# States renewed within the scan, turned states through the weight ring, twelve expert tiles loaded ahead, the light expert two blocks late, and packed weights

## The reference

```python
def mamba2(h, conv_buf, ssm_h, w_in, ...):
    proj = h @ w_in
    z = proj[..., :D_INNER]
    xbc, conv_new = causal_conv(proj[..., D_INNER:D_INNER + CONV_DIM], conv_buf, conv_w, conv_b)
    ...
    y, h_new = ssd(xs, dt, a_neg, bm, cm, ssm_h)      # chunked scan, per sequence state 32 x 64 x 128
    y = rmsnorm((y + d_skip[:, None] * xs).reshape(b, l, D_INNER) * jax.nn.silu(z), norm_g)
    return y @ w_out, conv_new, h_new
def moe(h, w_router, w_gate, w_up, w_down):           # 8 experts, D_MODEL 1024, D_FF_EXPERT 2816
    ...
    for e in range(N_EXPERTS):
        y = y + combine[..., e:e + 1] * swiglu(h, w_gate[e], w_up[e], w_down[e])
```

## Time and profile before

| | |
|---|---|
| median of 3 runs | 1618.4 us (1617.58 to 1619.77) |
| the profiled execution: time, span | 1623.92 us, 1622.1 us |
| TensorE busy | 1530.0 us (94%) |
| VectorE, ScalarE, GpSimd busy | 381.1, 277.4, 108.4 us |
| DMA traffic | 454.83 MB, mean 280 GB/s |
| expert stage, from the first expert product to the last | 909.84 to 1602.8 us |

### The profile page before, as it was taken

How to read it: one execution, slowest core, us unless ns; L and a number is a source line. 1 busy time by engine, 2 the same in 40 slices (tenths; PEclk the granted TensorE clock), 3 DMA queues, 4 the chain that set the end, 5 groups by cost and what they waited for, 6 DMA issues and landing times.

```text
span 1622.1 us, 24833 instructions
## 1 busy us (share of the span) xinstructions
PE 1530.0 (94%) x10024; PEld 906.4 (56%) x10024; DVE 381.1 (23%) x928; ACT 277.4 (17%) x618; POOL 108.4 (7%) x187
## 2 busy tenths in 40 slices
PE   7999988999999999999999999999999989998998
PEld 3545544678888878858787554553244234432342
DVE  2233422120000045644557300001000100011014
ACT  2122332110000022337612200000001000000001
POOL 0002424000000010011010200001000100010000
PEclk9999999899999999989999999999999999999999
DMA  9676972444433564564359999999999999999996
GB/s 373 268 239 238 395 234 71 156 125 137 155 110 123 182 194 134 156 204 142 92 200 369 320 337 374 390 398 392 414 403 417 395 411 406 418 394 406 411 411 223
DMA packets 195915, 454.83 MB, mean 280 GB/s; under 512 B 21870, under 2 KB 109963, under 8 KB 177845
## 3 DMA queue, kind: packets, MB, share of 16 engines
q1 hardware_dynamic: 181760, 406.07, 67.7%
q0 software_dynamic: 11536, 46.00, 8.2%
q10 hardware_dynamic: 2512, 1.23, 0.3%
HBM read 437.91 MB, written 15.55 MB: 280 GB/s over the span
## 4 chain that ended last, share of the span: by engine, by line
PE 80%; DMA 11%; DVE 5%; issue 2%; ACT 1%; SPq 0%; POOLq 0%; POOL 0%; DVEq 0%; ACTq 0%
PE bank L1056 11%; PE bank L1086 10%; PE bank L1546 9%; PE bank L1596 6%; DMA ring<-in_moe_w_up 6%; PE bank L1100 5%; PE bank L1439 5%; DMA ringx<-in_moe_w_up 3%; PE bank L1134 3%; PE bank L789 3%; PE bank L1454 2%; PE bank L1480 2%; PE bank L1558 2%; PE bank L823 2%; PE bank L876 1%
## 5 line engine op out<-in xcount | busy, mean ns | idle before, releaser
L1546 PE MATMUL bank<-ring,hg 128*32 128x512 f32 (+1 forms) x1456 | 208.4, 573 | 15.4 <-DMA ring<-in_moe_w_up 14.1
L1086 PE MATMUL bank<-hT,ring 128*128 128x264 f32 x704 | 156.9, 386 | 0.3 <-ACT hT L1649 0.3
L1546 PE MATMUL bank<-ringx,hg 128*32 128x512 f32 (+1 forms) x848 | 143.0, 558 | 7.3 <-DMA ring<-in_moe_w_up 5.2
L1086 PEld LDWEIGHTS bank<-hT,ring 128*128 128x128 f32 x704 | 133.7, 190 | 23.4 <-issue 0.6
L1546 PEld LDWEIGHTS bank<-ring,hg 128*32 128x32 f32 x1456 | 64.7, 112 | 118.9 <-issue 115.9
L1056 PE MATMUL bank<-hT,ring 128*128 128x264 f32 x512 | 118.7, 394 | 1.6 <-ACT hT L1649 1.3
L1056 PEld LDWEIGHTS bank<-hT,ring 128*128 128x128 f32 x512 | 99.1, 194 | 19.9 <-issue 2.1
L1596 PE MATMUL bank<-ring,turnH 128*32 128x512 f32 x768 | 90.9, 593 | 0.0
L1100 PE MATMUL bank<-actT,ring 128*128 128x264 f32 x352 | 79.1, 386 | 0.6 <-DVE actT L2139 0.6
L1546 PEld LDWEIGHTS bank<-ringx,hg 128*32 128x32 f32 x848 | 43.5, 111 | 62.9 <-issue 60.6
L1439 PE MATMUL bank<-ring,hg 128*128 128x512 f32 (+1 forms) x192 | 78.0, 560 | 0.6 <-ACT hg L1875 0.6
(11 more groups left out here) (562 smaller groups left out, 1843.4 us busy)
## 6 DMA issues: line engine op xcount, KB each, us to landing
ring<-in_moe_w_down SPq DMA_DIRECT2D x62, 1024.0 KB, 17.1
ring<-in_moe_w_up SPq DMA_DIRECT2D x51, 1024.0 KB, 17.0
ring<-in_w_ada SPq DMA_DIRECT2D x48, 1024.0 KB, 10.6
ring<-in_moe_w_gate SPq DMA_DIRECT2D x43, 1024.0 KB, 17.5
ringx<-in_moe_w_gate SPq DMA_DIRECT2D x27, 1024.0 KB, 13.9
ringx<-in_moe_w_down SPq DMA_DIRECT2D x26, 1024.0 KB, 18.2
ring<-in_ssm_w_in SPq DMA_DIRECT2D x20, 1024.0 KB, 5.3
ringx<-in_moe_w_up SPq DMA_DIRECT2D x19, 1024.0 KB, 16.8
```

The lines of the kernel that those rows point to most:

```text
L1086: m = mm(bank[2 * w + q][:, 0:T], slot8(tl)[:, k, q * P:(q + 1) * P], hT[:, k, :], start=k == 0, stop=k == DC - 1)
L1546: m = mm(bank[2 * b_ + u][rows, 0:HALVES[g][u]], hg[:, k, rows], w[:, kk, 512 * u:512 * u + HALVES[g][u]], start=k == 0, stop=k == DC - 1, ...
```

## The change

- State renewals stand within the scan: one in group 0 (`RENEWALS`), two in each of groups 1 to 3, the last behind the gated product. `st[:, 0]` takes the old state, `st[:, 1]` the new one; a renewal waits for the store of the one before it and for the load of its own.
- The turned states are tiles of the ring (`STT`, behind z tiles 0 and 1), and all eight `state_output` stand ahead of the scan.
- Twelve tiles of the first heavy expert are loaded ahead (`EARLY`), by the release of their slots; those of `ringx` by `gss_ready`. For this `ringx` lies elsewhere in SBUF.
- The light expert of the first pair goes two blocks behind the heavy one.
- All big weights but the adaLN ones are given in packed form, so that a partition's part of a tile is one run: 8 KB for the input projections, dense layer, output projection and first heavy expert, 8 KB and 6 KB for gate and up of pairs 1 to 3. The first pair's light expert keeps runs of 2 KB (gate, up) and 4 KB (down).
- The zero-fill of the result rows in memory moves from the router's stretch to GpSimd's time in the dense layer.

```diff
 RETURNS = (2, 0, 1)
+EARLY = (0, 1, 8, 9, 10, 11, 2, 3, 4, 5, 6, 7)
+RENEWALS = ((0,), (1, 2), (3, 4), (5, 6))
 KEPT = 7
 
 
...
 def first_events():
 
...
+AHEAD, PIECES = 12, 8
 
...
-        fill8(DTW, SH, wssm[:, :, 2 * DI + 2 * SG * SN:2 * DI + 2 * SG * SN + SH])
-        for j in range(8):
-            fill8(ZW + j, 256, wssm[:, :, 256 * j:256 * (j + 1)])
+            fill8(XBC + j, 256, wssm[:, 8 + j, :])
+        fill8(DTW, SH, wssm[:, 20, 0:DC * SH])
+        for j in range(2):
+            fill8(z_tile(j), 256, wssm[:, j, :])
+        for b in range(NB):
+            fill8(STT + b, 256, a["state_ssm_turned"][b])
+        for j in range(2, 8):
+            fill8(z_tile(j), 256, wssm[:, j, :])
         for j in range(8):
             n = WOUT + j
             sp.wait_ge(s["units"], unit(n - NS))
-            fill(n % NS, ring[:, n % NS, :].rearrange("p (c n) -> p c n", c=IC), wout_d[:, :, P * j:P * (j + 1)])
+            fill(n % NS, ring[:, n % NS, :], wout_d[:, j, :])
...
+        def first_tile(tile):
+
+
+            _, _, kind, g, i = tile
+            f0, width = GROUPS[g]
+            base = f0 * D + i * P * SLOT
+            return first_packed[kind][base:base + P * SLOT].rearrange("(p n) -> p n", p=P)
+
+        def packed_rows(kind, e, g, block):
+
+
+            (f0, width), rows = SUPER[g], PACK[g]
+            base = f0 * D + block * P * rows * width
+            return packed[kind][ds(e - 1, 1), base:base + P * rows * width].rearrange("a (p c n) -> (a p) c n", p=P, c=rows)
...
+            f0, width = SUPER[g] if p else GROUPS[g]
+            if not p and who == "heavy":
+                src = first_tile(tile)
+                dst = moe_slot(t)[:, 0:src.shape[1]]
+            elif kind == "down" and p:
+                src = md_rows[ds(e - 1, 1), :, f0 // 256 + i, :].rearrange("a p n -> (a p) n")
+                dst = moe_slot(t)
             elif kind == "down":
                 c0_ = f0 // P + 2 * i
-                src, rows, width = md[ds(e, 1), :, c0_:c0_ + 2, :], 2, D
+                src = md[ds(e - 1, 1), :, c0_:c0_ + 2, :].rearrange("a p c n -> (a p) c n")
+                dst = moe_slot(t).rearrange("p (c n) -> p c n", c=2)
+            elif p:
+                src = packed_rows(kind, e, g, i // (PACK[g] // 2))
+                src = src[:, i % (PACK[g] // 2) * 2:i % (PACK[g] // 2) * 2 + 2, :].rearrange("p c n -> p (c n)")
+                dst = moe_slot(t)[:, 0:2 * width]
             else:
-                rows = 2 if tile[0] else SLOT // width
-                src = (mg if kind == "gate" else mu)[ds(e, 1), :, rows * i:rows * (i + 1), f0:f0 + width]
-            sp.dma_start(moe_slot(t)[:, 0:rows * width].rearrange("p (c n) -> p c n", c=rows),
-                         src.rearrange("a p c n -> (a p) c n")).then_inc(moe_ready[t % MS], 16)
+                rows = SLOT // width
+                G0 = SUPER[g // 2][0]
+                src = packed_rows(kind, e, g // 2, i // (PACK[g // 2] // rows))
+                c0_ = i % (PACK[g // 2] // rows) * rows
+                src = src[:, c0_:c0_ + rows, f0 - G0:f0 - G0 + width]
+                dst = moe_slot(t).rearrange("p (c n) -> p c n", c=rows)
...
-        sp.wait_ge(s["st_ready"], NB - 2)
-        for t in range(FIRST):
-            sp.wait_ge(s["units"], unit(WOUT + t))
-            moe_load(MOE_TILES[t], 0)
-        sp.wait_ge(s["router_done"], 1)
-        for t in range(FIRST, AHEAD):
+        for t in EARLY:
+            if t < NS:
+                sp.wait_ge(s["units"], unit(WOUT + t))
+            else:
+                sp.wait_ge(s["gss_ready"], 4)
             moe_load(MOE_TILES[t], 0)
...
         g.wait_ge(s["rows_out"], 16)
+        g.memset(zrow[:], 0.0).then_inc(s["zeroed"], 1)
+        g.wait_ge(s["zeroed"], 4)
+        g.dma_start(xrow[1 + TP:1 + T, :], zrow[0:NB, :]).then_inc(s["rows_added"], 16)
+        g.dma_start(xrow[1:1 + TP, :].rearrange("(c p) d -> p c d", p=P), zrow[:].unsqueeze(1).to_broadcast([P, 2, D])).then_inc(s["rows_added"], 16)
+        g.wait_ge(s["rows_added"], 32)
...
         for i in range(NB):
             g.wait_ge(s["st_ready"], i + 1)
-            g.dma_start(oview[i], renewed[i % 4]).then_inc(st_stored[i % 4], 16)
-            if i < NB - 2:
-                g.dma_start(st[:, i % 2], sview[i + 2]).then_inc(st_loaded[i % 2], 16)
-        for i in range(4):
-            g.wait_ge(st_stored[i], 32)
+            g.dma_start(oview[i], st[:, 1]).then_inc(st_stored, 16)
+            if i < NB - 1:
+                g.dma_start(st[:, 0], sview[i + 1]).then_inc(st_loaded, 16)
+        g.wait_ge(st_stored, 16 * NB)
...
+        def state_output(b):
+
+
+            tile_ready(STT + b)
+            for g_ in range(SG):
+                m = mm(bank[3][32 * g_:32 * g_ + 32, :], cpad[:, g_, b, :], ring[:, (STT + b) % NS, 512 * g_:512 * (g_ + 1)],
+                       start=b == 0, stop=b == NB - 1, skip_group_check=True)
+            m.then_inc(s["units"], 2)
+
...
+        for b in range(NB):
+            state_output(b)
...
@@ -2231,13 +2242,13 @@
             if i == 0:
                 v.wait_ge(s["rows_spread"], 112)
                 v.wait_ge(s["us_silu"], 2)
-            v.wait_ge(st_loaded[i % 2], 16 * ((i + NB) // 2 + 1))
-            if i >= 4:
-                v.wait_ge(st_stored[i % 4], 16)
-            out, b = renewed[i % 4], i
+            if i:
+                v.wait_ge(st_stored, 16 * i)
+            out, b = st[:, 1], i
             shape = [P, IC, SN]
             link(v.tensor_tensor(out, srow[:, b, :].unsqueeze(1).to_broadcast(shape), xsp[:, b, :].unsqueeze(2).to_broadcast(shape), ALU.mult))
-            v.scalar_tensor_tensor(out=out, in0=st[:, i % 2], scalar=decay[:, b:b + 1], in1=out, op0=ALU.mult, op1=ALU.add).then_inc(s["st_ready"], 1)
+            v.wait_ge(st_loaded, 16 * (i + 1))
+            v.scalar_tensor_tensor(out=out, in0=st[:, 0], scalar=decay[:, b:b + 1], in1=out, op0=ALU.mult, op1=ALU.add).then_inc(s["st_ready"], 1)
...
             for n in range(4 * g_, 4 * g_ + 4):
                 weigh(n)
+                if n % 2 and n % 4 // 2 >= 2 - len(RENEWALS[g_]):
+                    state_renew(RENEWALS[g_][n % 4 // 2 - 2 + len(RENEWALS[g_])])
...
-        state_renew(0)
-        state_renew(1)
+        state_renew(NB - 1)
         v.wait_ge(s["gss_ready"], 4)
         v.wait_ge(s["gsq_ready"], 5)
         link(v.reciprocal(rstd[:], rvar[:]))
         for c in range(DC):
-            if c < DC - 2:
-                state_renew(c + 2)
             v.wait_ge(s["units"], unit(WOUT + c))
```

More of the change, by code:

```diff
@@ L71 @@
 COPIES = 2 * NG + 2 * NSG * (NP - 1)
-FIRST = 8
 RETURNS = (2, 0, 1)
+EARLY = (0, 1, 8, 9, 10, 11, 2, 3, 4, 5, 6, 7)
+RENEWALS = ((0,), (1, 2), (3, 4), (5, 6))
 KEPT = 7
 def first_steps():
-    return [(g if g < NG else None, g - 1 if g >= 1 else None) for g in range(NG + 1)]
+    return [tuple(g if 0 <= g < NG else None for g in (i, i - 1, i - 2)) for i in range(NG + 2)]
 def first_events():
-    return [(who, g) for hg_, lg in first_steps() for who, g in (("heavy", hg_), ("light", lg)) if g is not None]
+    return [(who, g) for hg_, hd_, lg in first_steps() for who, g in (("heavy", hg_), ("light", lg)) if g is not None]
 def moe_order():
@@ L100, in moe_order @@
     order = []
-    for hg_, lg in first_steps():
+    for hg_, hd_, lg in first_steps():
         if hg_ is not None:
             order += gate_up("heavy", hg_)
-        if lg is not None:
-            order += down("heavy", lg)
+        if hd_ is not None:
+            order += down("heavy", hd_)
         if lg:
@@ L540, in moe_load @@
         def moe_load(tile, e):
-            _, who, kind, g, i = tile
+            p, who, kind, g, i = tile
             t = MOE_AT[tile]
-            f0, width = SUPER[g] if tile[0] else GROUPS[g]
-            if kind == "down" and tile[0]:
-                src, rows, width = md_rows[ds(e, 1), :, f0 // 256 + i:f0 // 256 + i + 1, :], 1, SLOT
+            f0, width = SUPER[g] if p else GROUPS[g]
[5 more added lines that the diff above has]
+                dst = moe_slot(t)
@@ L1145, in _, with state_last @@
             m.then_inc(s["conv_turned"], 1)
+        def state_output(b):
[4 more added lines that the diff above has]
+            m.then_inc(s["units"], 2)
+        def state_last(g_):
+            if g_:
+                pe.wait_ge(s["hlast_copied"], g_)
+            else:
+                pe.wait_ge(s["xs_copied"], 2)
+            for q in range(4):
+                out = bank[3][:, q * P:(q + 1) * P]
+                mm(out, xdt[:, 3, q * P:(q + 1) * P], btok[:, 0, :], start=True, stop=False)
+                m = mm(out, xdt[:, 4, q * P:(q + 1) * P], btok[:, 1, :], start=False, stop=True)
+            m.then_inc(s["carry_done"], 1)
         pe.wait_ge(s["us_silu"], 1)
@@ L1508, in _ @@
                     indices(n, 0)
[L1509 removed]
+                if step == 1:
                     gather_light(r)
@@ L1880, in _ @@
             gathered(r, 0)
```

(2 more changed lines are left out.)

201 lines of the change are left out of this document (87 added, 114 removed).

## The result

The changed kernel takes 1625.3 us (median of 20 runs, 1621.6 to 1636.4), the kernel before 1619.3 (20 runs, 1616.4 to 1624.6): ratio 1.0035, 95% interval 1.002 to 1.005. It is slower by 5.7 us, where 9.2 us less was forecast, and it lies outside the range (1594 to 1619).

What follows compares the result with a forecast made beforehand. It took the expert weight stream to bound the last three pairs, TensorE the first pair and scan. Terms -3.5 + 10.0 + 4.0 - 1.7 - 10.2 - 8.8 + 1.0 = -9.2 us from 1618.4 gave 1609.2 us, range 1594 to 1619.

Steps and rivals of the forecast that it cites:

- the head start of the stream: First expert pair: more tiles landed ahead of TensorE, 3.5 tiles of 2.5 us, -8.8 us (bounds 0 and 12).
- The sign that the prediction names: Expert stream: some 8 or 9 tiles ahead when the second pair starts.
- the 2.5 us for a tile: Expert stream: each tile landed ahead of TensorE was counted as a gain of 2.5 us.
- One more step of the light expert: First expert pair: same products in one more step, light results turned without heavy gate work ahead, +1.0 us.
- States renewed in the scan: Scan: second renewals delay y, TensorE stalls 3.8, 3.8 and 2.4 us, +10.0 us (bounds 0 and 15).
- +4.0 of clock: Scan: two new TensorE stalls lower its clock, 2.0 us each, +4.0 us (bounds 0 and 6).
- Turned states and output projection: State products ahead of the scan without DMA wait, -3.5 us; no renewal before the output projection's first residual, -1.7 us.
- Packed weights: Last three expert pairs: longer contiguous runs raise the stream's rate, 3.4 us a pair, -10.2 us (bounds 0 and 12).
- The rival in which the stream does not gain: Expert stream: run length has no part, or the head start is lost; 1621 or 1618 us, chance 0.16.
- The slower rival: Scan: state traffic becomes the bound, deciding from a round trip of about 15 us; 1626 us, chance 0.08.

Runs made afterwards that it cites:

- e5: e4 with four expert tiles loaded ahead instead of ten; ratio 0.9903 to the kernel before.
- e4: The changed kernel with the edits of e1 and e3 together: light expert one block late, ten tiles ahead, one renewal a group; ratio 0.9908 to the kernel before.
- e1: The changed kernel with the first pair's light expert one block late and ten tiles ahead instead of twelve; ratio 0.9991 to the kernel before.
- e3: The changed kernel with one state renewal in each scan group, the other renewals behind the scan; ratio 0.9923 to the kernel before.
- e8: e3 with ten tiles ahead instead of twelve, light expert still two blocks late; ratio 0.9939 to the kernel before.
- e7: e4 with the weights in their old, unpacked layout; ratio 0.9971 to the kernel before.

## Why the prediction was wrong

**The step that failed is the head start of the stream**, forecast at -8.8 us. It put 4 to 6 tiles ahead at the second pair in the kernel before, and so saw room for 3.5 more, because it took all 203.5 MB of the windows for expert weights. There was no room: eleven tiles were out, seven of them landed, and 8 to 9 MB of the 207.6 had been moved, in before as in after. The sign that the prediction names, 8 or 9 tiles ahead at the second pair, came true and says nothing, since it was true already. It further reckoned the tiles ahead at the first pair's end as if what lies in the ring at its start, and each tile that faster packets bring, were still there 180 us later. But TensorE sets the pace in the first pair and never waits for a tile, so the ring refills from any start, and the stream then idles. e5, with four tiles ahead instead of ten, has the same time as e4, so the 2.5 us for a tile are 0 as far as the intervals tell (under 1 us). In place of a gain there is a loss: with the light expert two blocks late the stream has 0.7 to 0.9 MB more to move from pair 1 on in each of three comparisons (after to e1, e3 to e4, e8 to e4; last column), 1.7 to 2.2 us at 415 GB/s. The idle stream at the start of the pair, which I first took for the cause, is not it: e1 has 270 GB/s there and leaves 198.6 MB, while the packed kernels with the old order and a later head start leave 197.8 and 198.7. What remains is the order of the last tiles. The first tile of pair 1 takes the slot of the twelfth tile from the first pair's end; one block late, one of the eleven behind it is a heavy tile (its products take 3.60 us in e4, those of a light one 1.9), two blocks late all eleven are light ones. The first load of pair 1 goes out 26.4 us ahead of the pair's start in e1 and e4, and 24.7, 24.1 and 23.8 us in after, e3 and e8, which fits in size. In these three SyncE's load just ahead of it also took 3.47 us to issue, in e1 and e4 0.39 us. Which of the two makes the loss was not tested; no run changed these tiles alone.

**One more step of the light expert** (+1.0): 1.5 us of waits. With the lost lead the order costs 4 us by the ratios (2.4 from e3 to e4, 7.1 from after to e1).

**States renewed in the scan** (+10.0, and +4.0 of clock): mechanism, places and releasers as forecast; 10.9 and 3.8 us in the profile. By the ratios it is 18 us (after to e3) and 13 us (e1 to e4). The first product of after and e1 is at 918.6 us in the mean, that of the six kernels with one renewal at 901.7. So some 14 to 17 us; the term was mis-sized by up to 3. The round trip was 12.0, 11.1 and 10.7 us and not 10.6. That the forecast's 14.0 and the profile's 14.7 agree so well is in part luck: the three stalls came out at 4.9, 4.0 and 2.1 us, where 3.8, 3.8 and 2.4 were forecast, and the clock term was an estimate with bounds 0 and 6.

**Turned states and output projection** (-3.5 and -1.7, together -5.2): e7 gives -4.7 us in the median, and the first product of the six one-renewal kernels stands 6.0 us ahead of the mean of before's two.

**Packed weights** (-10.2): -10.2 us (e7 to e4), -10.9 us in their profiles. (The upper bound, 422 GB/s for all, works out at 12.8 us and not 12.) The rates by run length hold (399 GB/s with 3 KB runs, 416 with 6 KB), and the rule of the Trainium skill that I set against this term (page "DMA: Bandwidth & Descriptors", section "Specifications") does not give them: it has full rate from 512 B on.

Summed as measured: -5 to -6, +14 to +17, -10.2 and +4 make +2 to +6 us, where the forecast had -5.2 + 14.0 - 10.2 - 7.8 = -9.2. The measured 5.7 us lie within that, at its upper end. The rival in which the stream does not gain had the head start right and gave 1618 us for it. It was given 0.16, and stopped at zero; the loss from the order and up to 3 us of the scan make the rest. The slower rival's mechanism, a round trip of 15 us, did not occur.
